# Hybrid decoder layer on one core: the norm's row factor applied to each projected section instead of to x, with x loaded in quarters

## The reference, cut to what matters

```python
def rms_norm(x, w):
    y = x32 * lax.rsqrt(jnp.mean(x32 * x32, axis=-1, keepdims=True) + RMS_EPS)
    return (y * w).astype(x.dtype)

h = rms_norm(x, norm_w)                        # (1, 256, 2048)
proj = jnp.einsum('btd,de->bte', h, w_in)      # 2048 x 8204
# split into the sections of the three head groups; per head: q, k, v, gate
qkv = jax.nn.silu(causal_depthwise_conv(gqkv, conv_w))   # DeltaNet, 4 taps
g = -exp(a_log) * softplus(ga + dt_bias);  beta = sigmoid(gb)
...
return x + jnp.einsum('bte,ed->btd', y, w_out)
```

## Time and profile before

| | |
|---|---|
| median of 3 runs | 561.47 us |
| the profiled execution | 561.29 us, of it the span 559.5 us |
| granted clock, mean | 0.997 |
| PE busy | 97% of the span |
| DVE busy | 332.7 us (59%) |
| ACT busy | 282.7 us (51%) |
| POOL busy | 89.1 us (16%) |
| HBM traffic | 163 GB/s over the span |

### The profile page before, as it was taken

The page is one execution under the profiler, slowest core; times in us unless marked ns, Lnnn a source line. Parts: engine busy times, 40 slices in busy tenths (PEclk is TensorE's granted clock), DMA queues, the critical chain, the costliest instruction groups (busy, mean ns, idle before and its releaser), DMA issues.

```text
span 559.5 us, 8847 instructions
## 1 busy us (share of the span) xinstructions
PE 543.0 (97%) x3456; PEld 465.6 (83%) x3456; DVE 332.7 (59%) x524; ACT 282.7 (51%) x457; POOL 89.1 (16%) x94
## 2 busy tenths in 40 slices
PE   3999999998999999999999999999999999999997
PEld 3887888887888878888888988888888888888885
DVE  2776886767678597446464356475456447655451
ACT  4766654445544653355654554564455546433340
POOL 1002122012230112111221121132131212000000
PEclk9999999998999999999999999999999999999999
DMA  9997654555345554546387648747765656487711
GB/s 276 205 294 169 186 151 122 144 131 134 76 114 152 150 134 118 153 125 174 90 213 203 175 122 229 185 116 189 188 163 151 180 185 189 159 273 222 230 56 37
DMA packets 149931, 91.81 MB, mean 164 GB/s; under 512 B 7843, under 2 KB 139138, under 8 KB 149762
## 3 DMA queue, kind: packets, MB, share of 16 engines
q1 hardware_dynamic: 148562, 88.95, 58.8%
q10 hardware_dynamic: 1328, 2.31, 1.2%
HBM read 89.13 MB, written 2.10 MB: 163 GB/s over the span
## 4 chain that ended last, share of the span: by engine, by line
PE 93%; ACT 3%; DMA 1%; DVE 1%; issue 0%; POOL 0%; ACTq 0%
PE pj L1132 37%; PE pj L1133 18%; PE pj L1154 5%; PE pj L1151 5%; PE pj L1153 5%; PE pj L1192 3%; PE pj L1129 2%; PE mx L1293 2%; PE mx L1303 2%; DMA cst<-table_dram 1%; PE pj L1197 1%; PE mx L1280 1%; PE pj L1128 1%; PE mx L1270 1%; PE mx L1182 1%; ACT w_hi L345 1%
## 5 line engine op out<-in xcount | busy, mean ns | idle before, releaser
L1132 PE MATMUL pj<-hT,w_hi 128*128 128x512 f32 x900 | 330.4, 406 | 0.0
L264 DVE TENSOR_TENSOR w_lo<-w_raw,w_hi 128x1024 fp32r<-128x1024 f32 x160 | 202.7, 1276 | 104.4 <-ACT w_hi L345 103.9
L1133 PE MATMUL pj<-hT,w_lo 128*128 128x256 f32 x900 | 252.3, 280 | 0.0
L345 ACT ACTIVATE w_hi<-w_raw 128x1024 fp32r<-128x1024 f32 x160 | 168.0, 1055 | 99.5 <-PE pj L1133 62.0
L1132 PEld LDWEIGHTS pj<-hT,w_hi 128*128 128x128 f32 x900 | 169.2, 188 | 37.3
L1133 PEld LDWEIGHTS pj<-hT,w_lo 128*128 128x128 f32 x900 | 170.1, 189 | 2.3
L658 POOL TENSOR_TENSOR raw<-ev 128x256 f32<-128x256 f32 x64 | 56.4, 882 | 322.0 <-ACT ev L353 321.9
L353 ACT ACTIVATE ev<-pj 128x512 f32<-128x512 f32 x64 | 37.9, 594 | 68.2 <-PE pj L1129 66.0
L1151 PE MATMUL pj<-w_hi,yT 128*128 128x512 f32 x128 | 50.3, 393 | 0.0
L1154 PE MATMUL pj<-w_lo,yT 128*128 128x512 f32 x128 | 49.9, 389 | 0.0
L1153 PE MATMUL pj<-w_hi,yT 128*128 128x512 f32 x128 | 49.8, 389 | 0.0
(11 more groups left out here) (206 smaller groups left out, 448.0 us busy)
## 6 DMA issues: line engine op xcount, KB each, us to landing
w_raw<-in_w_in_dram SPq DMA_DIRECT2D x256, 256.0 KB, 3.4
w_raw<-in_w_out_dram SPq DMA_DIRECT2D x64, 256.0 KB, 3.6
big<-in_x_dram SPq DMA_DIRECT2D x8, 256.0 KB, 5.3
out_dram<-sq ACTq DMA_DIRECT2D x8, 256.0 KB, 4.5
big<-in_x_dram SPq DMA_DIRECT2D x1, 1024.0 KB, 5.1
big<-in_x_dram SPq DMA_DIRECT2D x2, 512.0 KB, 7.7
cst<-table_dram SPq DMA_DIRECT2D x1, 682.0 KB, 4.6
cst<-table_dram ACTq DMA_DIRECT2D x1, 196.0 KB, 7.4
```

What stands on the lines that cost most here:

```text
L264: eng.tensor_tensor(w_lo[:, n % NSPLIT, :], w_raw[:, n % NRAW, :], w_hi[:, n % NSPLIT, :].bitcast(F32), ALU.subtract).then_inc(S("lo"), 1)
L345: act.activation(w_hi[:, n % NSPLIT, :], w_raw[:, n % NRAW, :], ACT.Copy).then_inc(S("hi_done"), 1)
L1132: pe.matmul(pj[s][:, :], high, hT[:, kc].rearrange("p a t -> p (a t)"), start=first, stop=False)
L1133: ins = pe.matmul(pj[s][:, 0:T], low, hT[:, kc, 0, :], start=False, stop=False)
```

## The change

The row factor is no longer multiplied into x. The transposed x goes into the projections with `norm_w` alone; POOL multiplies each section by `rb`, the factor of every token laid along the free axis and repeated on all partitions (two TensorE transposes into PSUM, one DVE copy), after it has added the halves. `abT` gets the same product on DVE, which takes it over from ACT. The sums of squares are taken during group 0, 512 columns at a time, ACT for tokens 0 to 127, DVE for the others. The identity is a DMA of its own, first on ACT's queue; x is loaded in four quarters, the first two by ACT, the others by SP between weight tiles; the rest of the parameters is issued by ACT during group 0. Taps are issued 9 units after a section's end instead of 6, and ACT's `advance(U_FIRST + 7)` is new.

```diff
-TAP_AFTER = 6
+TAP_AFTER = 9
...
+        rb = sb("rb", [P, T])
...
+        def load_quarter(eng, i):
+            piece = slice(i * 4 * P, (i + 1) * 4 * P)
+            for c in range(C):
+                eng.dma_start(x_sb[:, c, piece], x[0, c * P:(c + 1) * P, piece]).then_inc(S(f"x_in{i}"), 16)
...
-            sp.dma_start(x_sb[:, 0, :], x[0, 0:P, :]).then_inc(S("x0_in"), 16)
-            for i in range(2):
-                half = slice(i * D // 2, (i + 1) * D // 2)
-                sp.dma_start(x_sb[:, 1, half], x[0, P:T, half]).then_inc(S(f"x1_in{i}"), 16)
...
             for n in range(TILES):
                 load(n)
+                if n in (1, 4):
+                    load_quarter(sp, 2 + n // 4)
...
+            act.dma_start(cst[:, 0:P], table[:, 0:P]).then_inc(S("ident_in"), 16)
             act.dma_start(prow[R_NORM:R_CONV, :], norm_w[0].rearrange("(k p) -> k p", p=P)).then_inc(S("norm_in"), 16)
-            act.dma_start(cst[:, 0:K_FIRST], table[:, 0:K_FIRST]).then_inc(S("cst_in"), 16)
+            load_quarter(act, 0)
+            load_quarter(act, 1)
+            act.dma_start(cst[:, P:K_FIRST], table[:, P:K_FIRST]).then_inc(S("cst_in"), 16)
...
+            act.wait_ge(S("norm_cols"), 1)
             for b in range(KC // 2):
-                act.wait_ge(S("norm_cols"), 1)
                 act.wait_ge(S("hT_psum"), b + 1)
                 for k in range(2 * b, 2 * b + 2):
                     act.activation(hT[:, k, 0, :], mx[b % 4][:, k % 2 * T:(k % 2 + 1) * T], ACT.Copy,
                                    scale=pcol[:, R_NORM + k:R_NORM + k + 1]).then_inc(S("h_hi"), 1)
-                if b == 0:
-                    scale_first(1)
-                if b < 2:
-                    high_part(b + 1)
+                if b < LEAD:
+                    high_part(b)
                 else:
-                    advance(UPT * (b - 1))
-                if b in (1, 3):
-                    scale_first((b + 3) // 2)
+                    advance(UPT * (b - LEAD + 1))
+                if b % 2:
+                    square_sum(b // 2)
+                if b in (2, 3, 4, 5):
+                    load_params(b - 2)
...
-            act.wait_ge(S("abt_psum"), 1)
-            act.activation(abT, mx[0][0:32, :], ACT.Copy).then_inc(S("abt_done"), 1)
...
             square_first(0)
+            advance(U_FIRST + 7)
             tanh_kq(0, 1)
...
-                pool.tensor_tensor(raw[:, g % 2, s, PAD:], ev[:, n % 2, 0:T], ev[:, n % 2, T:2 * T], ALU.add).then_inc(S("evac"), 1)
+                pool.tensor_tensor(ev[:, n % 2, 0:T], ev[:, n % 2, 0:T], ev[:, n % 2, T:2 * T], ALU.add).then_inc(S("halves"), 1)
+                if n == 0:
+                    pool.wait_ge(S("rb_done"), 1)
+                pool.wait_ge(S("halves"), n + 1)
+                pool.tensor_tensor(raw[:, g % 2, s, PAD:], ev[:, n % 2, 0:T], rb[:, :], ALU.mult).then_inc(S("evac"), 1)
...
+            dve.wait_ge(S("ss_act"), 4)
+            dve.wait_ge(S("ss_vec"), 4)
+            dve.tensor_reduce(sm[:, 8:10], sm[:, 0:8].rearrange("p (c i) -> p c i", c=C), AX.X, ALU.add).then_inc(S("ss2"), 1)
+            dve.wait_ge(S("ss2"), 1)
+            dve.tensor_scalar(sm[:, 10:12], sm[:, 8:10], 1.0 / D, EPS, ALU.mult, ALU.add).then_inc(S("ms_done"), 1)
             dve.wait_ge(S("wab_hi_done"), 1)
             dve.tensor_tensor(wab_lo, wab[:, :, :], wab_hi.bitcast(F32), ALU.subtract).then_inc(S("wab_lo_done"), 1)
+            dve.wait_ge(S("rb_psum"), 1)
+            dve.tensor_copy(rb[:, :], mx[3][:, 0:T]).then_inc(S("rb_done"), 1)
+            dve.wait_ge(S("rb_done"), 1)
+            dve.wait_ge(S("abt_psum"), 1)
+            dve.tensor_tensor(abT.rearrange("p (a t) -> p a t", a=2), mx[0][0:32, :].rearrange("p (a t) -> p a t", a=2),
+                              rb[0:32, :].unsqueeze(1).broadcast_to([32, 2, T]), ALU.mult).then_inc(S("abt_done"), 1)
             advance(66)
...
-            keep_busy(14)
-            pe.wait_ge(S("x0_scaled"), 1)
-            for b in range(2):
-                x_blocks(b, 0)
-            keep_busy(6)
-            pe.wait_ge(S("x1_scaled"), 1)
-            for b in range(2):
-                x_blocks(b, 1).then_inc(S("hT_psum"), 1)
-            keep_busy(8)
+            keep_busy(12)
+            for b in range(2):
+                pe.wait_ge(S(f"x_in{b // 2}"), 16 * C)
+                for c in range(C):
+                    ins = x_blocks(b, c)
+                ins.then_inc(S("hT_psum"), 1)
+            keep_busy(10)
...
+            pe.wait_ge(S("rstd_done"), 1)
+            for c in range(C):
+                ins = pe.transpose(mx[3][:, c * P:(c + 1) * P], sm[:, 6 + c:7 + c].broadcast_to([P, P]), ident)
+            ins.then_inc(S("rb_psum"), 1)
```

More of the change, by code:

```diff
@@ L389, in advance, with square_sum, load_params @@
                 pos[0] = max(pos[0], u)
[L392 to L412 removed]
+            def square_sum(i):
+                if i:
+                    act.wait_ge(S("ss_act"), i)
+                act.activation(junk_a[:, 0:4 * P], x_sb[:, 0, i * 4 * P:(i + 1) * 4 * P], ACT.Square,
+                               accum_out=sm[:, i:i + 1]).then_inc(S("ss_act"), 1)
+            def load_params(i):
+                if i == 0:
+                    act.dma_start(wab[:, :, :], w_in[0, :, AB_COL:AB_COL + AB].rearrange("(k p) c -> p k c", p=P)).then_inc(S("wab_in"), 16)
+                elif i == 1:
+                    act.dma_start(prow[R_CONV:R_RET, :], conv_w[0].rearrange("j (t c) -> (j t) c", c=P)).then_inc(S("param_in"), 16)
+                elif i == 2:
+                    act.dma_start(prow[R_RET:R_GDN, :], ret_norm_w[0]).then_inc(S("param_in"), 16)
+                    act.dma_start(prow[R_GDN:R_Q, :], gdn_norm_w).then_inc(S("param_in"), 16)
+                else:
+                    act.dma_start(prow[R_Q:R_K, :], q_norm_w).then_inc(S("param_in"), 16)
+                    act.dma_start(prow[R_K:R_ROWS, :], k_norm_w).then_inc(S("param_in"), 16)
+            act.wait_ge(S("norm_cols"), 1)
             for b in range(KC // 2):
[L415 removed]
                 act.wait_ge(S("hT_psum"), b + 1)
@@ L628, in _ @@
             pool.wait_ge(S("cst_in"), 16)
-            for c in range(C):
-                pool.wait_ge(S("ms_done"), c + 1)
-                power(6 + c, 10 + c, 1).then_inc(S("rstd_done"), 1)
+            pool.wait_ge(S("ms_done"), 1)
+            power(6, 10, 2).then_inc(S("rstd_done"), 1)
             def split_y(p, y0):
@@ L1240, in _ @@
             pe.wait_ge(S("abt_done"), 1)
+            pe.wait_ge(S("cst_in"), 16)
             pe.wait_ge(S("cst_in2"), 16)
```

60 lines of the change are left out of this document (10 added, 50 removed).

## The result

The changed kernel took 574.77 us (median of four runs, 572.95 to 577.49) against 561.29 for the kernel before: a ratio of 1.024, interval 1.021 to 1.028. It is slower by 13.5 us. I had forecast slower, but by 3.4 us, and the time lies outside my range of 559.2 to 568.5. The profiled execution is the slowest of the four, 577.49 us with a span of 575.7; it ran at a mean granted clock of 0.982, the other three at 0.984 to 0.990.

What follows compares the result with a forecast made beforehand. TensorE, busy for 543.0 of 559.5 us, was taken to bound the kernel. The sum was 561.29 - 5.2 (start) + 6.6 (group 1) + 1.2 + 1.0 (pair ends) = 564.9 us, with a range of 559.2 to 568.5.

Steps and rivals of the forecast that it cites:

- The start's gain of 5.2: Kernel start: the first product comes at 10.6 instead of 15.84 us, a gain of 5.2 us.
- part 3: POOL's multiply hidden, costing nothing; later taps at the first and second DeltaNet pair ends cost 1.2 and 1.0 us.
- rival 3: The slow clock: one or two of the new waits bring half clock, 566.6 to 568.3 us; chance 0.10.
- My own sign: First product to first line 1270, 53.5 us before: the forecast is wrong if this stays below 56.
- the bound 13: Kernel start: latest first product, 13 us, if the first quarter lands like a 512 KB load in a full queue.
- Group 1, +6.6 forecast: Group 1: VectorE's queue delays TensorE, the main loss, 6.6 us, bounds 4.0 to 8.0.
- (a): Start of group 1: VectorE waits for abt_psum before low parts 8 to 10; unit 64 starts 2.4 late, +1.8 us.
- (b): Group 1, around the cumulated decays: low parts, parameter copy, taps and convolution come late; TensorE loses 2.05 us.
- (c): Group 1, near v = 120: the later tap stands behind squares and high part, delaying low part 15; +2.75 us.
- Rival 1: The helpers keep up, VectorE having more slack in group 1: faster, 559.0 us, between 557.9 and 560.1; chance 0.22.
- The pair ends: Ends of the first and second DeltaNet pairs: later taps lengthen TensorE's waits, +1.2 and +1.0 us.
- rival 4: POOL and DVE slow each other beside low parts 8 to 10 in group 1: +2 to +3, 567.4 us; chance 0.06.

Runs made afterwards that it cites:

- a4: Changed kernel with a one-column activation before ScalarE's first wait and the second half of x quarter 0 issued by SyncE ahead of its weights: 572.22 us.
- a1: Changed kernel with transposes of the identity in each of TensorE's waits of over a microsecond behind group 0: 571.14 us.
- a3: Changed kernel with VectorE's low parts of tiles 8 to 10 issued before its wait for abt_psum: 576.55 us.
- a5: Changed kernel without GpSimd's multiply, so the row factor is missing from the sections; tap distance still 9: 570.06 us.
- a6: Changed kernel without GpSimd's multiply (row factor missing from the sections) and with the tap distance back at 6: 564.28 us.
- a8: Changed kernel, tap distance 9, GpSimd's add writing the section and a same-size multiply behind it into an unread buffer; row factor left out: 573.77 us.
- a7: c1 with GpSimd's multiply left out, and so the row factor missing from the sections: 557.31 us.
- c1: c2 with VectorE's low parts 8 to 10 made before its wait for the abT products: 564.06 us.
- c2: Changed kernel with tap distance 6, the two start edits of a4, and 16 and 12 spare transposes at the ends of pairs 1 and 2: 564.32 us.
- b1: Kernel before the change with 16 spare identity transposes in TensorE's wait at the end of the first DeltaNet pair: 559.86 us.
- a2: Changed kernel with the tap distance back at 6 units instead of 9: 569.11 us.

## Why the forecast was wrong

The direction held, the size did not. On the axis of the two profiled executions my sum was +3.6 and the loss 16.1; by the medians it was 3.4 and 13.5. Three terms failed. The start's gain of 5.2 was 2.1 in the profiled execution. The multiply on POOL, which part 3 put at nothing, was worth 4.7 us. The clock, which the sum leaves out and rival 3 has at 0.10, fell in four places instead of one. My own sign, the distance from the first product to the first sums of squares, was 62.4 us, where the sum had 60.1; it bears out that group 1 is late. A part of the clock is in the prices of the other two, so that the three can't be added up to the whole.

**The start, -5.2 forecast, -2.1 measured.** The norm weights landed at about 5, near my 4.5. Two things failed in this term. The first quarter of x landed at 9.45 and not near 6.3, so that TensorE, which I had ready for it at 7.4, lost 2.1. The timeline of the changed kernel at its start:

```profile
1.76 3.44 ACTq L272 DMA_DIRECT2D big<-in_x_dram  x4
...
9.45 1.97 PE L1169 MATMUL mx<-cst,big 128*128 128x128 f32 x8 [1.46 <-DMA big<-in_x_dram]
...
10.65 1.28 ACT L416 ACT_TABLE_LOAD   x1 [10.65 <-PE mx L1169]
...
13.78 1.43 PE L1186 MATMUL pj<-hT,w_hi 128*128 128x512 f32 x5 [0.60 <-ACT w_hi L345]
```

I had taken 5.1 us for a megabyte from the earlier trace rows, where it was the first thing in an empty queue. Here the four issues of x alone hold ScalarE's queue for 3.44 us, and a piece of 256 KB took a median of 7.4 from issue to landing. And the change takes away ScalarE's first activation at the start, the sum of squares of x, whose table load cost nothing. The timeline of the kernel before has it ahead of the wait for x:

```profile
1.66 1.28 ACT L396 ACT_TABLE_LOAD   x1 [1.66 <-PEq L1477]
...
5.89 1.06 ACT L396 ACTIVATE kq<-big 128x1024 f32<-128x1024 f32 x1 [2.95 <-DMA big<-in_x_dram]
```

In the changed kernel it stands behind ScalarE's wait for the first transposes, 1.28 us on the path. I had the bound 13 for the first; the second I missed, and 13.78 lies past my bound. 2.1 and 1.3 make the 3.2 that were short, within 0.2. a4 got 1.9 back with both edits, which it doesn't tell apart. Nor is -2.1 a fixed number. Seven profiled executions have the changed kernel's start (after, a1 to a3, a5, a6, a8): their first product is at 13.31 to 14.69, and their `wab` products, when group 0 is done, at 38.90 to 40.57, against 40.98 before. That is a gain of 0.4 to 2.1, 1.1 in the mean; a part of it is lost in group 0 (25.36 to 26.08 for 25.14), for which my sum had nothing. With the start mended (a4, a7, c1, c2) they are at 36.66 to 37.27, a gain of 3.7 to 4.3.

**Group 1, +6.6 forecast, +8.7 measured.** The waits came as I had listed them, and nearly as long:

| step | forecast | measured |
|---|---|---|
| (a) first product of group 1 late, wait there | 2.1 | 1.97, and the 0.6 before `abT` gone |
| (b) wait before the cumulated decays | 1.4 | 1.37 |
| (b) wait behind them for low part 11 | 0.65 | 0.37 |
| (c) wait near v = 120 for low part 15 | 2.75 | 2.29 |
| (c) idle of VectorE before the last convolution | 2.2 | 2.05 |

With the 0.6 taken off they make 5.4 (the last row is VectorE's idle time behind the same loss and isn't counted), less than my 6.6. The other 3.3 are half clock behind (b) and around (c), 5.3 us of it, worth an estimated 2.7 by half of its length, and 0.6 that I can't place. Rival 1, that the helpers keep up, fell: VectorE was at low part 11 after TensorE was at the decays.

**The pair ends, +1.2 and +1.0 forecast, +4.8 and +1.8 measured, and +1.9 behind them.** The wait at the first was 4.03 instead of my 3.35; the second 1.74 for 1.8. The timeline of the changed kernel has the missing 0.7:

```profile
139.38 2.39 DVE L781 SCALAR_TENSOR_TENSOR big<-raw,pcol,big 128x256 f32<-128x256 f32 x3 [1.51 <-ACT big L364]
...
139.90 0.72 POOL L654 TENSOR_TENSOR ev<-ev 128x256 f32<-128x256 f32 x1 [0.93 <-ACT ev L353]
...
140.71 0.79 POOL L658 TENSOR_TENSOR raw<-ev,rb 128x256 f32<-128x256 f32 x1
...
143.75 1.87 PE L1266 MATMUL mx<-cst,sq 128*128 128x1 f32 x8 [4.03 <-ACT sq L481]
```

The three convolution steps take 2.39 us beside an add and a multiply, 1.53 in the earlier trace rows. That is the collision of rival 4 at a place where I had not looked for it, and the multiply is the smaller part of it: in a5, beside the add alone, they take 2.05, and the wait is 3.70.

The larger part is the clock, rival 3, to which I gave 0.10. From the first sums of squares on, the table is 4.8, 1.8 and 1.9 us worse; the waits account for 1.9 and 0.9 of it (4.03 for 2.15, 1.74 for 0.81), half of the additional length at half clock for about 2.4, 1.1 and 1.7 (4.9, 2.3 and 3.4 us of it). I had argued from two waits of before, one of 2.15 us with half clock behind it and one of 0.81 without, and had priced one or two falls more; four of the changed kernel's stretches are at half clock, two of them 6.8 us long. The step that failed is the chance, and the length: I took 1.7 us each. Why these are twice as long as the others stays open. In all, the trace has 17 us more at half clock than before, an estimated 8.5 us by half of their length. a1 says how much of that is to be had back: 3.6, since TensorE then waits for helpers instead; and b1 got 1.9 back from the kernel before in the same way. So the clock is a large part of this one execution's loss and a small part of the change's: with the spare transposes in both kernels 11.3 of 13.5 us are left.

**The multiply on POOL, "nothing" in my part 3.** Its time is hidden, as I said, and its price is not. (The mean of 0.88 that I took from the earlier trace rows is not in them, which have a median of 742 ns; it is the line's 56.4 us of busy time over 64.) The line that I had read (median 742, worst 1748 ns for line 658; worst 2182 for line 264) has this answer in the changed kernel: duration in ns, least, median and longest.

```profile
L658 POOL TENSOR_TENSOR raw<-ev,rb x64: 731/743/4157, 40.6 to 484.4; 128x256 f32<-128x256 f32 x64
```

The median hasn't moved, the longest is 4157. I had rival 4 at 0.06 and at 2.5 us. a5 and a6 put the whole multiply at 4.7 and 4.8 with the changed kernel's other causes there, a8 its load alone at 3.7, and a7 against c1 the whole at 6.75 with those causes mended. I had looked for it only among four operations at the start of group 1. It is spread over the low parts that meet one: 12.6 us of VectorE's time in a8, most of them hidden. What comes on the path is shown by itself only behind the DeltaNet pairs, where TensorE loses 0.7 to 1.0 us.

**The tap.** My (c) and the pair ends put about 2.3 + 1.2 + 1.0 us on it; a2 measured 5.7, clock included.

**Range and chances.** The range allowed two extra falls of the clock on top of the forecast, but not together with rival 4 and a short start. These aren't alternatives: a short gain at the start, slowed helpers and half clock can all come in one execution. That tap and multiply add is shown by a5 and a6. (The range's lower end, 559.2, is called the upper end of rival 1, whose own numbers were 557.9 to 560.1.)

## What to carry to other kernels

Work that moves to an idle GpSimd is not free when VectorE is the helper that sets TensorE's pace: price it by what it does to VectorE's instructions that meet it, not by GpSimd's share. When a change adds waits of one to four microseconds on a TensorE that was never idle, look at the granted clock behind each, and let transposes of a constant fill the wait. When the first activation of ScalarE is removed or moved, look where its table load comes to stand (here from 1.66 us, idle, to 10.65, on the path); a dummy activation ahead of the first wait put it at 4.27. When the clock differs between executions of one kernel, compare medians, and fill the waits in both kernels before saying what the clock cost.

## What the runs showed of the hardware

- A GpSimd multiply of two SBUF operands that began at 43.67 us, 0.08 before the first of three low parts on VectorE, ended after the last of them, 4.16 us later, while the three took 3.47 together. In a3 and c1, where GpSimd's instruction is an add of 0.74 alone, it took 1.70 to 1.80 and the low parts 4.58. So in the first case one engine was held for several instructions of the other, and in the second both lost. The Trainium skill, page "SBUF — State Buffer", section "SBUF: two separate sides", says that whichever of the two starts first keeps the shared port for its whole instruction. The second case doesn't contradict it; in the first, the GpSimd instruction started first in the trace and was the one that was held.
- Half clock doesn't follow every wait of the same length. It followed 2.15 us at 132 in the kernel before, 1.97 at unit 64 in a5, a6 and c2, and 1.37 and 0.37 in the changed kernel; it did not follow 2.15 us at the first pair end in a2 and a6, nor 1.97 at unit 64 in the changed kernel, a2 and a8. So a change's price in half clock can differ from one execution to the next: the four times of the changed kernel spread over 4.5 us and their mean clock from 0.982 to 0.990. Those of c1 and c2, where the waits at the pair ends are filled, spread over 0.4 and 0.2, but those of b1 over 3.2.
- Sixteen transposes in the wait of b1 kept TensorE at full clock, in products that follow them and in the windows (0.50 before, 1.00 in b1); that is the profiled execution, and in three of nine the mean clock stayed at 0.997.
- The table load took 1.28 us in each trace, wherever it stood. The Trainium skill, page "ScalarE activation tables: per-element evaluation and per-set limits", section "What a function is on this engine", gives 1283 ns for it; the trace agrees.
- Some 0.6 us in group 1 and 0.5 at the first pair end are in neither the waits nor the clock; their cause stays open.
